# A state-space part whose decay matrices are built from rows spread by DMA and masked on GpSimd instead of by TensorE products

## The chip, the cores and the metric

The kernel is one program for one core of a Trainium2 chip. It runs three whole transformer-like blocks on 256 tokens of width 1024. The metric is the device time in microseconds, the median of several runs. TensorE (PE in the profile) multiplies matrices, VectorE (DVE) and ScalarE (ACT) do elementwise work, GpSimd (POOL) does some elementwise work and issues a few DMAs, SyncE (SP) issues all weight loads.

## The reference, cut to the state-space mixer

```python
dt = softplus(dt_raw + dt_bias); a = dt * (-exp(a_log))            # 32 heads
acum = cumsum(a)
seg  = acum[:, :, None] - acum[:, None, :]
lmat = exp(where(causal, seg, -inf))                               # decay, per head
xdt  = xc * dtc[..., None]
cb   = einsum('btgn,bsgn->btsg', cc, bc)                           # scores, per group
y    = einsum('btsg,btsgr,bsgrp->btgrp', cb, lmat, xdt)            # 8 groups of 4 heads
y    = (y + d_skip * xs) * silu(z)
y    = y * rsqrt(mean(y*y over a group) + EPS) * norm_g            # then @ w_ssd_o
```

The chunk length covers all 256 tokens, so the state terms vanish. A head is 64 channels wide, a group of four heads 256. The scores are kept with the source token on the partitions: 128 source tokens by 256 targets for the first half, 128 by 128 for the second, 384 columns in all.

## The kernel before

Everything is fp32. A weight piece of 128x1024 is split into a high and a low half: ACT copies the high half (`halves<-raw`, L2896), DVE subtracts to get the low one (L1543), and PE runs three products (hi·hi, hi·lo, lo·hi). Pieces live in a ring of four, so the high half of piece n+4 waits until PE has read piece n. Each engine has one instruction stream, executed in order, and the order is written out by hand: a wait at the head of a stream holds up all that is behind it, splits of weights included.

The part in question (`mix2`) starts when PE has finished the convolution's projection (16 tiles, pieces of L585, L586 and L589) and goes on to the gate projection `m2.gb`: eight pieces of 12 products each (L659). The state-space work is laid between these pieces in three blocks, by generators called `ssm` on PE, DVE and ACT that are advanced 22 steps before pieces 2, 4 and 6 and finished after piece 7. The first half of the gate projection fills PSUM banks 1 and 2; ACT copies them out after its split at step 3 (L3486), and piece 4 waits for it.

For each group g of four heads:

- PE computes the scores `cb` into a PSUM bank (L1150, L1151), and for each head a product with a selecting vector (L1157) that spreads the row of cumulated decays over 128 partitions, with a second product that adds the causal mask (L1158). The rows come in three parts (`acx`), made by DVE with `in_three` during the convolution.
- ACT takes the exponential with a bias from PSUM to SBUF (L3448 on 256 columns, L3449 on 128).
- DVE copies the scores to SBUF (L2328) and multiplies decay, step size and scores, two instructions a head (L2336).
- PE sums over the source tokens (L1167 to L1169, 24 products a group).
- DVE adds the skip term (L2348) and multiplies with silu(z) (L2355), ACT squares and sums (L3455), DVE finishes the mean (L2379), GpSimd raises it to the power -1/2 (`inverse_root`, L1426), DVE scales (L2362).

When all eight groups are scaled, PE transposes them (`turn` "m2.n", L567, 32 transposes), and the product with `w_ssd_o` begins (L659 with `R` as the moving side).

ACT may start its exponentials after the last silu of the convolution (L3415) and a table load (L3440). The cumulated rows are there when the scan on DVE ends (L2291), far ahead, within the convolution. SP's queue holds weight loads only, each waiting for a raw buffer.

## Time and profile before

| what | value |
|---|---|
| median of 3 runs | 2816.58 us (2816.2 to 2816.72) |
| span of the profiled execution | 2814.9 us |
| PE busy over the span | 2800.3 us, 99% |
| DVE, ACT, POOL busy | 1952.1 us, 1624.4 us, 345.9 us |
| TensorE clock granted | full in all slices |

PE is busy nearly throughout, but a product's duration is more than the step to the next one, so a busy PE isn't PE at its peak. The stretch of this change lasts from 1332.20 us (first piece of the gate projection) to 1393.27 us (first transpose) and 1397.09 us (first product of `w_ssd_o`). In a timeline a row is: start, duration, engine, line, operation, output and input, count, and in brackets the idle time ahead with what ended it.

### The profile page before, as it was taken

What the parts mean: (1) busy time and instruction counts of PE and PEld (TensorE: products, weight loads), DVE (VectorE), ACT (ScalarE), POOL (GpSimd) and SP (SyncE); (2) the same over time, 40 slices, a digit from 0 to 9 for tenths busy, and PEclk for the clock granted to TensorE, in tenths of its full rate; (3) what the DMA queues carried; (4) which work ended last, traced back from release to release, by engine and by line L of the source; (5) the groups of instructions that cost most, each with busy time, mean ns of one, the idle gap of its engine ahead of it and who ended that gap; (6) DMA issues with size and microseconds to landing.
All of it is one profiled execution on the core that took longest, in us unless ns stands there. A gap on an engine that the chain in (4) does not pass through costs nothing.

```text
span 2814.9 us, 42397 instructions
## 1 busy us (share of the span) xinstructions
PE 2800.3 (99%) x16834; PEld 2485.0 (88%) x16834; DVE 1952.1 (69%) x3377; ACT 1624.4 (58%) x2784; POOL 345.9 (12%) x314
## 2 busy tenths in 40 slices
PE   9999999999999999999999999999999999999999
PEld 7888888888988888899889999999888889988997
DVE  6657765776676676768866998677555566766775
ACT  6544655755665564566745445776555555655663
POOL 0000000000010002000002445894000000000000
PEclk9999999999999999999999999999999999999999
DMA  7554556466436555445164554434555574536454
GB/s 229 191 178 159 181 194 227 135 202 221 148 124 194 202 189 181 135 156 187 61 224 166 183 182 160 136 131 161 193 192 193 194 246 137 180 110 209 147 195 149
DMA packets 270485, 491.25 MB, mean 175 GB/s; under 512 B 10880, under 2 KB 181248, under 8 KB 261584
## 3 DMA queue, kind: packets, MB, share of 16 engines
q1 hardware_dynamic: 268864, 480.08, 51.3%
q0 software_dynamic: 1424, 8.45, 0.8%
q8 instruction: 135, 2.21, 0.3%
q14 instruction: 62, 0.51, 0.1%
HBM read 486.41 MB, written 2.10 MB: 174 GB/s over the span
## 4 chain that ended last, share of the span: by engine, by line
PE 94%; DVE 4%; ACT 1%; issue 0%; DMA 0%; POOL 0%; DVEq 0%; POOLq 0%; ACTq 0%
PE ps L659 41%; PE ps L747 11%; PE ps L589 8%; PE ps L585 8%; PE ps L586 8%; PE ps L746 6%; PE ps L606 3%; PE ps L1268 2%; DVE halves L1543 1%; PE ps L1303 1%; PE ps L544 1%; DVE AR L2499 1%; PE ps L952 0%; PE ps L1322 0%; DVE AR L2495 0%
## 5 line engine op out<-in xcount | busy, mean ns | idle before, releaser
L2896 ACT ACTIVATE halves<-raw 128x1024 fp32r<-128x1024 f32 x828 | 870.1, 1058 | 695.5 <-PE ps L659 413.7
L1543 DVE TENSOR_TENSOR halves<-raw,halves 128x1024 fp32r<-128x1024 f32 x790 | 952.9, 1227 | 190.6 <-ACT halves L2896 187.4
L659 PE MATMUL ps<-halves,XX 128*128 128x512 f32 x2628 | 611.6, 391 | 0.4
L659 PEld LDWEIGHTS ps<-halves,XX 128*128 128x128 f32 x2628 | 489.9, 188 | 102.5 <-DVE XX L1581 1.0
L585 PE MATMUL ps<-XX,halves 128*128 128x256 f32 (+1 forms) x1960 | 486.1, 286 | 0.0
L586 PE MATMUL ps<-XX,halves 128*128 128x256 f32 (+1 forms) x1960 | 480.3, 283 | 0.0
L659 PE MATMUL ps<-halves,R 128*128 128x512 f32 x1908 | 439.9, 390 | 0.1
L659 PEld LDWEIGHTS ps<-halves,R 128*128 128x128 f32 x1908 | 356.7, 188 | 73.9 <-issue 0.6
L586 PEld LDWEIGHTS ps<-XX,halves 128*128 128x128 f32 (+1 forms) x1960 | 375.4, 192 | 0.1
L585 PEld LDWEIGHTS ps<-XX,halves 128*128 128x128 f32 (+1 forms) x1960 | 375.0, 191 | 0.1
L747 PE MATMUL ps<-XX,halves 128*128 128x512 f32 x1344 | 338.4, 393 | 0.6 <-DVE XX L1581 0.6
L747 PEld LDWEIGHTS ps<-XX,halves 128*128 128x128 f32 x1344 | 241.7, 189 | 44.5 <-ACT halves L2896 0.9
L589 PE MATMUL ps<-XX,halves 128*128 128x256 f32 (+1 forms) x1960 | 275.3, 283 | 0.2 <-DVE halves L1543 0.2
L589 PEld LDWEIGHTS ps<-XX,halves 128*128 128x128 f32 (+1 forms) x1960 | 252.7, 192 | 0.4 <-DVE halves L1543 0.4
L746 PEld LDWEIGHTS ps<-XX,halves 128*128 128x128 f32 x1344 | 183.2, 190 | 13.4 <-issue 0.4
L746 PE MATMUL ps<-XX,halves 128*128 128x256 f32 x1344 | 187.5, 282 | 0.1
L1426 POOL TENSOR_TENSOR st<-st 128x1 f32<-128x1 f32 x44 | 25.3, 574 | 1182.0 <-DVE st L1608 1001.9
L1431 POOL TENSOR_TENSOR halves<-raw,halves 128x1024 fp32r<-128x1024 f32 x38 | 97.0, 2552 | 435.3 <-ACT halves L2896 435.3
L1558 DVE TENSOR_TENSOR XX<-AR,XX 128x256 fp32r<-128x256 f32 x127 | 53.9, 426 | 137.9 <-ACT XX L3579 137.9
L1509 POOL TENSOR_SCALAR raw<-iota,xsel 128x128 f32<-128x128 f32 x128 | 137.5, 1081 | 34.5 <-PE ps L1268 22.4
L1807 DVE TENSOR_TENSOR AR<-AR,ps 128x256 f32<-128x256 f32 x164 | 68.5, 421 | 81.1 <-ACT AR L3096 81.1
L3096 ACT ACTIVATE AR<-ps 128x256 f32<-128x256 f32 x164 | 61.3, 375 | 89.4 <-PE ps L747 88.0
(390 smaller groups left out, 3180.8 us busy)
## 6 DMA issues: line engine op xcount, KB each, us to landing
raw<-in_w_ffn_in SPq DMA_DIRECT2D x88, 1024.0 KB, 5.1
raw<-in_w_in SPq DMA_DIRECT2D x74, 1024.0 KB, 5.3
raw<-in_uT SPq DMA_DIRECT2D x64, 1024.0 KB, 4.9
raw<-in_peer_v SPq DMA_DIRECT2D x64, 1024.0 KB, 4.9
raw<-in_w_ffn_out SPq DMA_DIRECT2D x44, 1024.0 KB, 4.9
raw<-in_w_up SPq DMA_DIRECT2D x24, 1024.0 KB, 5.8
raw<-in_mlstm_w_in SPq DMA_DIRECT2D x12, 1024.0 KB, 5.2
raw<-in_w_down SPq DMA_DIRECT2D x12, 1024.0 KB, 4.9
```

What stands on the lines that cost most here:

```text
L585: mm(o[:, ts], hi[:, q, 0:M], xh[:, k0 + q, ts], start=first and q == 0, stop=False)
L586: mm(o[:, ts], hi[:, q, 0:M], xl[:, k0 + q, ts], start=False, stop=False)
L589: ins = mm(o[:, ts], lo[:, q, 0:M], xh[:, k0 + q, ts], start=False, stop=last and q == a - 1)
L606: ins = mm(ps[:, bs[j], :].rearrange("p (a b) -> p a b", b=128), act[q == 2][:, t, j * 128:(j + 1) * 128], k.halves[:, 0:4, q % 2, t * 128 ...
L659: ins = mm(ps[:, bs[j * (width // 512) + h], :], xv[:, k0 + t, j * 128:(j + 1) * 128], wv[:, t, h * 512:(h + 1) * 512], start=first and q ...
L746: mm(o[:, 0:256], lo[:, p, :], X[0][:, p, :], start=False, stop=False)
L747: ins = mm(o.rearrange("p (h t) -> p h t", t=256), hi[:, q, :], k.XX[:, :, q, :], start=q == 0, stop=q == 7)
L1431: nc.gpsimd.tensor_tensor(lo, src, hi.bitcast(F32), ALU.subtract).then_inc(k.lo_pool, 1)
L1509: nc.gpsimd.tensor_scalar(OA[:, g % 2, q, :], k.iota[:], ih1[:, 4 * g + q:4 * g + q + 1], gw[:, 4 * g + q:4 * g + q + 1], ALU.is_equal, AL ...
L1543: te.tensor_tensor(lo, src, hi.bitcast(F32), ALU.subtract).then_inc(k.lo_made, 1)
L1807: te.tensor_tensor(dst, dst, o[:, 0:256], ALU.add) \
L2896: act(hi, src, ACT.Copy).then_inc(k.hi_made, 1)
```

## The change

1. **Decay rows.** PE's products L1157 and L1158 are gone (64 instructions), and DVE's `in_three` with them. GpSimd writes the 32 rows of cumulated decays to HBM (two DMAs), and reads them back spread over 128 partitions, 4 rows of 384 columns a group (768 KB), into a ring of four buffers. Buffer g % 4 is refilled after PE's sums of group g - 4.
2. **Mask.** GpSimd masks each group with two `affine_select` of 128x4x128.
3. **Exponentials** read and write SBUF, eight instructions a group as before, but the four heads are marked together.
4. **Scores** are copied by ACT instead of DVE. DVE multiplies four heads at once, one instruction of 128x1536, and puts the step sizes into x, one of 128x512 (`stepped`).
5. **Scaling** of groups 0 to 5 moves from DVE to GpSimd, groups 6 and 7 stay.
6. **Order.** The generators are gone. `SSM_STEPS` says how many groups are begun by gate piece i: 0, 1, 2, 4, 5, 7, 8, 10. PE takes scores of group n and sums of group n - 2 ahead of piece i, DVE and ACT after their split for step i. Sums use the banks that the decays had, so the score banks serve scores alone.

GpSimd's stream, before (with the neighbours) and now. `AR` is the big buffer in SBUF, `rows` the new tensor in HBM; `var` is DVE's mean, `mm` PE's sums, `pow` GpSimd's own root.

```order
L1426 TENSOR_TENSOR AR<-AR,st 128x16
L1426 TENSOR_TENSOR AR<-AR,st 128x16 [waits var]
L1426 TENSOR_TENSOR AR<-AR,st 128x16
L1426 TENSOR_TENSOR AR<-AR,st 128x2 [waits var] x8
L1426 TENSOR_TENSOR st<-st 128x1 [waits x_var] x2
```

```order
L1491 DMA AR<-rows 128x1536 [waits mm]
L1497 AFFINE_SELECT AR<-AR 128x4x128 [waits dma_decay_in0]
L1497 AFFINE_SELECT AR<-AR 128x4x128
L1491 DMA AR<-rows 128x1536 [waits mm]
L1419 TENSOR_TENSOR AR<-AR,st 128x2 [waits var]
L1505 TENSOR_SCALAR AR<-AR 128x256 [waits pow]
L1505 TENSOR_SCALAR AR<-AR 128x256
L1497 AFFINE_SELECT AR<-AR 128x4x128 [waits dma_decay_in1]
L1497 AFFINE_SELECT AR<-AR 128x4x128
L1491 DMA AR<-rows 128x1536 [waits mm]
```

Eight roots in a row become a stream in which the refill of group 5 stands behind the mask of group 4, and the mask of group 5 behind root and scaling of group 0.

ACT's stream at the step of gate piece 3, before and now. L3455 (now L3486) are the squares, L3448 and L3449 (now L3467 and L3468) the exponentials, L3480 the copy of the scores, L3511 (L3486 before) the copy of gate banks 1 and 2, L2896 (now L2919) the split.

```order
L3448 ACTIVATE AR<-ps,AR 128x256 [waits mm]
L3449 ACTIVATE AR<-ps,AR 128x128
L2896 ACTIVATE halves<-raw 128x1024 [waits piece_read]
L2896 ACTIVATE halves<-raw 128x1024 [waits piece_read,raw0_in]
L3486 ACTIVATE AR<-ps 128x512 [waits piece_read]
L3486 ACTIVATE AR<-ps 128x512
L3448 ACTIVATE AR<-ps,AR 128x256 [waits mm]
```

```order
L3480 ACTIVATE AR<-ps 128x384 [waits mm,prob]
L3467 ACTIVATE AR<-AR 128x256 [waits pool]
L3468 ACTIVATE AR<-AR 128x128
L3467 ACTIVATE AR<-AR 128x256
L3468 ACTIVATE AR<-AR 128x128
L3467 ACTIVATE AR<-AR 128x256
L3468 ACTIVATE AR<-AR 128x128
L3467 ACTIVATE AR<-AR 128x256
L3468 ACTIVATE AR<-AR 128x128
L3486 ACTIVATE AR<-AR 128x256 [waits part]
L3486 ACTIVATE AR<-AR 128x256
L3511 ACTIVATE AR<-ps 128x512 [waits piece_read]
```

The wait on `pool` in the second row is the mask of group 4; squares of group 0 and the copy of the gate banks stand behind it now.

The new constants and buffers:

```diff
+SSM_STEPS = (0, 1, 2, 4, 5, 7, 8, 10)
+POOL_SCALED = 6
...
+    def decays(self, g):
+        return self.ar(8192 + g % 4 * 1536, 4, 384)
+    def stepped(self, g):
+        return self.ar(14336 + g % 2 * 512, 2, 256)
```

On PE (the rest of the old `ssm` generator is gone too):

```diff
-        def decay(h):
-            b = aux.take(pe, ("m2", "L", h))
-            mm(ps[:, b, 0:384], bc(k.sel[0:96, h:h + 1], [96, 128]), acx, start=True, stop=False)
-            ins = mm(k.diagonal(b), identb[:], mkq, start=False, stop=True)
...
+        for i, until in enumerate(SSM_STEPS):
+            for n in range(done, until):
+                if n < 8:
+                    group(n)
+                if n >= 2:
+                    sums(n - 2)
```

On GpSimd:

```diff
+    def spread(g):
+        if g >= 4:
+            gp.wait_ge(*k.full["m2", "ssm", g - 4])
+        load(k.decays(g), k.rows[4 * g:4 * g + 4, :].partition_broadcast(128))
+    def masked(g):
+        gp.wait_ge(*dma[f"decay_in{g % 4}"].need(g))
+        for o in (0, 256):
+            L = k.decays(g)[:, :, o:o + 128]
+            ins = nc.gpsimd.affine_select(L, L, [[0, 4], [1, 128]], ALU.is_ge, NEG, base=0, channel_multiplier=-1)
+    for g in range(4):
+        spread(g)
+    for g in range(4):
+        masked(g)
+    for g in range(9):
+        if g < 4:
+            spread(g + 4)
+        if g:
+            n = 2 * g - 2
+            inverse_root(cc[:, 144 + n:146 + n], cc[:, 128 + n:130 + n], s["var"].need(("m2.g", g - 1)), ("m2.g", g - 1))
+        if 1 <= g <= POOL_SCALED:
+            scaled(g - 1)
+        if g < 4:
+            masked(g + 4)
```

On DVE, whose order for each n is: `group(n)`, `sums(n - 2)`, `stepped(n)`, `moment(n - 3)`, and `scale(n - 4)` from n = 10 on:

```diff
-            for j, o in enumerate((slice(0, 256), slice(256, 384))):
-                ins = te.scalar_tensor_tensor(L[:, o], L[:, o], cc[:, 32 * j + h:32 * j + h + 1],
-                                              cbs[:, h // 4 % 2, o], ALU.mult, ALU.mult)
+            te.tensor_tensor(k.decays(g), k.decays(g), bc(cbs[:, g % 2, :].unsqueeze(1), [128, 4, 384]), ALU.mult)
```

On ACT:

```diff
+        def ssm(n):
+            if n < 8:
+                score(n)
+            if n < 7:
+                group(n + 1)
+            if 3 <= n < 11:
+                sums(n - 3)
...
+        group(0)
+        for i, until in enumerate(SSM_STEPS):
             weights()
+            for n in range(done, until):
+                ssm(n)
```

## Rows read from the trace of the kernel before

**Rows 1.** The page: busy time of each engine over the span

```profile
PE 2800.3 (99%) x16834; PEld 2485.0 (88%) x16834; DVE 1952.1 (69%) x3377; ACT 1624.4 (58%) x2784; POOL 345.9 (12%) x314
```

**Rows 2.** Windows: length, busy time by engine (instructions), clock, DMA share, GB/s

```profile
1300.00:1332.00 32.00, 32.00 (x269) 32.00 (x268) 26.25 (x45) 19.20 (x27) 0.00 (x0) 1.00 0.61 200
1332.20:1393.27 61.07, 59.88 (x386) 51.20 (x385) 54.26 (x150) 39.74 (x112) 5.81 (x8) 1.00 0.22 70
1393.27:1397.09 3.82, 3.74 (x34) 3.41 (x32) 3.82 (x7) 3.75 (x11) 0.00 (x0) 1.00 0.03 8
```

**Rows 3.** Timeline of PE in the stretch

```profile
1332.20 5.63 PE L659 MATMUL ps<-halves,XX 128*128 128x512 f32 x24
1337.67 0.59 PE L1150 MATMUL ps<-AR 128*128 128x256 f32 x2
...
1338.24 0.42 PE L1157 MATMUL ps<-R,sel 96*128 96x384 f32 x1
...
1338.55 0.42 PE L1157 MATMUL ps<-R,sel 96*128 96x384 f32 x1
...
1342.92 0.33 PE L1167 MATMUL ps<-AR 128*128 128x64 f32 x2
...
1345.54 0.65 PE L1150 MATMUL ps<-AR 128*128 128x256 f32 x2
```

**Rows 4.** Groups, 1337 to 1400 us: count, busy, mean ns, idle before

```profile
L3448 ACT ACTIVATE AR<-ps,AR 128x256 f32<-128x256 f32 x32 | 15.8, 492 | 11.3 <-PE ps L1158 11.3
L2336 DVE SCALAR_TENSOR_TENSOR AR<-AR 128x256 f32<-128x256 f32 x32 | 15.4, 480 | 1.9 <-ACT AR L3449 1.1
...
L2348 DVE SCALAR_TENSOR_TENSOR AR<-AR,ps 128x128 f32<-128x128 f32 x32 | 8.9, 343 | 0.8 <-PE ps L1169 0.8
...
L1426 POOL TENSOR_TENSOR AR<-AR,st 128x2 f32<-128x2 f32 x8 | 5.8, 726 | 279.4 <-DVE AR L2379 279.4
L2355 DVE TENSOR_TENSOR AR<-AR 128x512 f32<-128x512 f32 x8 | 5.5, 692 | 0.3
```

**Rows 5.** Timeline of ACT around its first exponentials and the gate copy

```profile
1336.58 1.28 ACT L3440 ACT_TABLE_LOAD   x1
...
1337.98 1.99 ACT L2896 ACTIVATE halves<-raw 128x1024 fp32r<-128x1024 f32 x2
1339.88 0.46 ACT L3448 ACTIVATE AR<-ps,AR 128x256 f32<-128x256 f32 x1
...
1340.49 0.47 ACT L3448 ACTIVATE AR<-ps,AR 128x256 f32<-128x256 f32 x1
...
1357.98 1.08 ACT L3486 ACTIVATE AR<-ps 128x512 f32<-128x512 f32 x2 [1.59 <-PE ps L659]
...
1359.56 0.43 ACT L3455 ACTIVATE AR<-AR 128x256 f32<-128x256 f32 x1
...
1360.27 0.22 ACT L3455 ACTIVATION_READ_ACCUMULATOR AR<-AR 128x1 f32 x1
```

**Rows 6.** GpSimd's lines: duration in ns, min/median/max

```profile
L1511 POOL TENSOR_SCALAR raw<-iota,xsel x64: 595/598/1681, 1734.3 to 1939.4; 128x128 f32<-128x128 f32 x64
...
L1431 POOL TENSOR_TENSOR halves<-raw,halves x38: 2397/2410/3717, 12.1 to 2593.0; 128x1024 fp32r<-128x1024 f32 x38
```

**Rows 7.** Timelines of GpSimd and DVE where both run

```profile
1745.76 2.58 POOL L1509 TENSOR_SCALAR raw<-iota,xsel 128x128 f32<-128x128 f32 x2 [0.52 <-PE ps L1268]
...
1753.30 1.65 POOL L1509 TENSOR_SCALAR raw<-iota,xsel 128x128 f32<-128x128 f32 x2 [0.81 <-PE ps L1268]
...
1746.37 1.22 DVE L1543 TENSOR_TENSOR halves<-raw,halves 128x1024 fp32r<-128x1024 f32 x1
```

**Rows 8.** The page and the DMA view: KB each, median us from issue to landing

```profile
spill<-AR POOLq DMA_DIRECT2D x1, 1024.0 KB, 5.2
...
AR<-in_rpack POOLq DMA_DIRECT2D x2, 512.0 KB, 7.0
```

**Rows 9.** Timeline of DVE: the scan that gives the decay rows

```profile
1272.11 0.69 DVE L2291 TENSOR_TENSOR_SCAN AR<-AR 96x256 f32<-96x256 f32 x1
```

More of the change, by code:

```diff
@@ L317, in __init__ @@
         (self.raw, self.halves, self.AR, self.part_at, self.XX, self.XF, self.cols, self.ident,
[L318 removed]
+         self.identb, self.sel, self.iota, self.mask, self.st, self.xsel, self.first, self.ps, self.spill, self.rows) = mem
         self.X = (self.XX[:, 0], self.XX[:, 1])
@@ L1200, in mix2 @@
                     k.full["m2.gb", s0, j] = k.piece_read, n + 1
-        pe.finish()
-        turn("m2.n", xs, lambda c, j: s["chan"].need(("m2", c // 2, j)), n=16, banks=k.late)
+        turn("m2.n", xs, lambda c, j: (s["pool"] if c // 2 < POOL_SCALED else s["chan"]).need(("m2", c // 2, j)),
+             n=16, banks=k.late)
         mix = k.ar(17408, 2, 1024)
@@ L2292, in dt_rows @@
             yield
-            acx = k.part_at(26112, 384)[0:96, :]
-            v.wait_ge(*step.need("m2.rows"))
-            in_three(acx[:, 0:256], ac)
             yield
-            te.tensor_copy(acx[:, 256:384], acx[:, 128:256].bitcast(F32)).then_inc(*step.mark("m2.acx"))
             yield
@@ L3442, in decay, with group, score @@
         def decay(h):
[L3443 to L3450 removed]
+            L = k.decays(h // 4)[:, h % 4, :]
+            act(L[:, 0:256], L[:, 0:256], ACT.Exp, bias=cc[:, 64 + h:65 + h])
+            return act(L[:, 256:384], L[:, 256:384], ACT.Exp, bias=cc[:, 96 + h:97 + h])
+        def group(g):
+            a.wait_ge(*s["pool"].need(("m2.L", g)))
+            a.wait_ge(*aux.gone(("m2", "cols")))
+            ins = [decay(h) for h in range(4 * g, 4 * g + 4)][-1]
+            ins.then_inc(*s["act"].mark(("m2.L", g)))
+        def score(g):
+            if g >= 2:
+                a.wait_ge(*s["prob"].need(("m2.L", g - 2)))
+            a.wait_ge(*full["m2", "cb", g])
+            act(cbs[:, g % 2, :], ps[:, k.right.of(("m2", "cb", g)), 0:384], ACT.Copy) \
+                .then_inc(*k.right.done(("m2", "cb", g)))
         def sums(g):
```

179 lines of the change are left out of this document (73 added, 106 removed).

## The prediction

> **What bounds the kernel now.** The page comes first: PE is busy for 99% of the span [rows 1], so the question is what the one stretch that changes costs PE. The windows give its length: 61.07 us from the first gate piece to the first transpose and 3.82 us of transposes, 64.89 us together; PEclk stands at 1.00, so the clock plays no part, and GpSimd does 5.81 us in all of it [rows 2]. PE's timeline gives the steps, not the durations, since products overlap. Two gate pieces take 1337.67 - 1332.20 = 5.47 us, so 2.74 each; scores of a group 1338.24 - 1337.67 = 0.57; a head's decay pair 1338.55 - 1338.24 = 0.31; a group's sums 1345.54 - 1342.92 = 2.62 [rows 3]. So PE's own work before the transposes is 8 x 2.74 + 8 x 0.57 + 32 x 0.31 + 8 x 2.62 = 21.9 + 4.6 + 9.9 + 21.0 = 57.4 us of 61.07. DVE is busy for 54.26 of the 61.07, ACT for 39.74 [rows 2]: near its end PE is paced by DVE, which waits little. ACT does wait, 11.3 us for PE's masked rows [rows 4].
>
> **What goes.** The decay pairs leave PE: 9.9 us, and with them most of the remaining 3.7 us of waits could go. PE's floor becomes 47.5 us, 13.6 us under today; that is the most that this change could give. DVE loses the multiplications per head (15.4 us for the 256-column form alone [rows 4]), the score copies and six scalings, and gets per group one product of 1536 columns and one of 512. The latter is 0.69 [rows 4]; 1024 columns take 1.22 [rows 7], so a column costs 1.03 ns and 1536 of them about 1.75 us, an estimate. 8 x 2.44 = 19.5 us: DVE stops being a bound by its own work. ACT gets eight score copies of about 0.5 us. `in_three` leaves DVE in the convolution, where PE has no idle time in a window of 32.00 us [rows 2]: worth nothing.
>
> **What hides.** The rows are ready at 1272.8 [rows 9], 59 us ahead of the stretch. Two stores, four refills and eight masks fit in there: even at the dearest prices below, one after the other (5.2 for the stores as for a 1024 KB one [rows 8], 4 x 8, 8 x 2.4), that is 56 us. The refills add 3 MB to weight loads with DMA share 0.61 [rows 2]; I cost that at nothing, because ACT and not the transfer paces the splits there. If the cover failed, it would cost the few us by which a weight load came late.
>
> **What comes on the path.** Only groups 0 to 3 are prepared ahead. For 4 to 7 the order on GpSimd and ACT makes a chain, which I follow from t = 0 at 1332.20.
>
> (a) ACT used to split right behind the table load, at 1337.98 [rows 5], t = 5.8. Now the exponentials of group 0 stand there: 4 x 0.61 = 2.44 (1340.49 - 1339.88 a head), then two splits, 1.90 [rows 5]. DVE's product of group 0 stands behind the split of a piece that needs the first of these, and needs ACT's score copy behind both: 5.8 + 2.4 + 1.9 + 0.5 = 10.6. Product 1.75, step sizes 0.69, sums 2.62: 15.7, with five handovers of 0.1 us 16.2. PE has nothing else by then and idles about 3 us.
>
> (b) The refill of group 4 waits for these sums. 768 KB: 1024 KB from the same queue took 5.2 us, two spread rows of 512 KB together 7.0 [rows 8]. I take 5.5, nearer the single transfer, range 4.5 to 8. Then the mask, which no row shows. A 128x128 tensor-scalar takes 0.60 us; 128x1024 with two inputs takes 2.41, half of that is 1.2 for 512 columns [rows 6]. Bounds for one instruction are 0.6 (as the 128-column one) and 2.4 (four times that); I take 1.1, so 2.2 a group. Group 4 is masked at t = 16.2 + 5.5 + 2.2 = 23.9.
>
> (c) ACT stands at the exponentials of group 4 meanwhile. Behind them in its stream are the squares of group 0 and the copy of the gate banks, for which PE waits with piece 4. And on GpSimd the mask of group 5 stands behind root and scaling of group 0, which need those squares. So from mask to mask the path is: exponentials 2.5, squares 0.9 (1359.56 to 1360.49 [rows 5]), mean 0.16, root 0.73 [rows 4], two scalings of 256 columns of about 0.8 (0.6 for 128 [rows 6], and twice the columns), mask 2.2, handovers 0.5: 8.6 us. The refill beside it is 5.5 + 2.2 = 7.7, just shorter. Three such periods lead to group 7.
>
> (d) GpSimd slows beside DVE. A pair of its instructions took 1.65 us alone and 2.58 with one DVE subtraction of 1.22 us in it [rows 7]: 0.9 us. DVE is in instructions with two SBUF inputs for about half of this stretch, so I add 1.0 us to each period and to the first mask.
>
> Mask 7 ends at 23.9 + 1.0 + 3 x 9.6 = 53.7.
>
> (e) Then exponentials 2.5, squares 0.9, split 1.0, score copy 0.5, product 1.75, and ahead of the step sizes of group 7 DVE has four skip additions (1.1) and one product (0.69) [rows 4], then the step sizes 0.69: with handovers 9.6, t = 63.3. Sums 2.62, piece 7 2.74: 68.7. Transposes 3.8, and 0.5 for gate banks that ACT empties late: 73.0.
>
> Against 64.89 that is +8.1 us. The same counting on the old order came out 1 to 2 us above its trace, so my handovers are a little dear; I take +7. Nothing outside the stretch changes. The profiled span was 2814.9 us against a median of 2816.58; the difference of 1.7 stays, so 2816.6 + 7 = **2823.6 us**.
>
> **Two pages against the rows.** That two DVE and GpSimd instructions disturb each other is in [rows 7]. The Trainium skill, SBUF — State Buffer, section "SBUF: two separate sides", has it that the shared port pair is an exclusive lock held for a whole instruction, against DVE instructions with two SBUF inputs. The stretched pair agrees with that; taken to the letter, a mask would wait for all of a 1.75 us product, and the sum would be about +10. The Trainium skill, GPSIMD Engine Reference, section "Performance versus the Vector engine", gives 769 ns for 512 elements in its best case; masks at that price would be 0.7 us cheaper a group and the sum about +4.
>
> **The rivals.**
>
> *It becomes faster.* GpSimd decides: four masks and three periods lie on the path. If the two masks of a group cost 1.2 us (the lower bound) and DVE doesn't slow them, a period is 7.6 and the first mask ends at 22.9; mask 7 ends at 45.7, 8 us ahead of the forecast, and PE's own queue (s4 to s7 with pieces 5 to 7) takes up half of it: -1 to -4 us, 2813.5. The point at which it turns is a period of about 7.6 to 7.8 us instead of 9.6. For it speaks that only exponentials and squares, 3.4 us, are fixed; against it, [rows 7]. Chance 0.12.
>
> *Masks as I price them, little contention.* Subtract 1.0 x 4 us and the handovers: +2 to +4, 2819.5. For it: root and scaling are short, and DVE itself waits in each period. Chance 0.30.
>
> *The refill decides.* If 768 KB spread over partitions takes 8 us (two of 512 KB together took 7.0), the first mask comes 2.5 us later, and each period is 10.2 + 1.0 of contention instead of 9.6: +14, 2831. Chance 0.12.
>
> *The mask is dear.* At 2.4 us an instruction, 2.6 more for each of four groups: +17, 2834. Chance 0.08.
>
> Forecast: 0.38.
>
> **How the numbers follow.** A measurement of this kernel tells 0.2%, 5.6 us, from no change. The forecast's own spread is +4 to +11, with 0.27 of its 0.38 above 5.6; with both dear cases this gives slower 0.47. The little-contention case and the rest are within, and most of the gain in the fast rival is too (its far end of -4 isn't enough, so a real gain needs more than I count): same 0.43, faster 0.10. The range reaches from the fast rival to the refill case, 2813 to 2833.
>
> **What would show it.** Right: PE has no L1157 or L1158 rows; it idles before the first sums, before gate piece 4 (waiting for ACT's copy) and most before the last sums, 6 us or more; ACT waits three or four times for GpSimd, 3 to 6 us each; GpSimd's masks come 9 to 10 us apart. DVE idles where it was full. Wrong: masks below 0.7 us or a period below 8 us; a refill above 7 us; PE waiting before the first four groups, which would mean that the preparation isn't hidden; or idle time of PE within the convolution.

## The result, and the profile after

| | before | after |
|---|---|---|
| median, us (4 runs each) | 2816.65 | 2831.26 |
| lowest to highest, us | 2816.2 to 2816.85 | 2831.18 to 2833.16 |
| profiled span, us | 2814.9 | 2829.4 |
| mean granted clock | 1.0 | 0.994 |

The changed kernel is slower by 14.6 us: a ratio of 1.0054 (from the single runs, not from the two medians), 95% interval 1.004 to 1.0068. The forecast was 2823.6 in a range of 2813 to 2833: the direction and the range held, the forecast loss of 7 us was half of what came.

All of it lies in the stretch that the prediction followed. Below are the windows of the changed kernel (length, busy time of PE, PEld, DVE, ACT, POOL with instructions, granted clock, DMA share, GB/s): the convolution ahead of the stretch, the stretch up to the first transpose, and the transposes up to the first product of `w_ssd_o`.

```profile
1300.00:1332.00 32.00, 32.00 (x269) 32.00 (x268) 26.26 (x44) 18.96 (x27) 0.00 (x0) 1.00 0.64 206
1331.96:1406.35 74.39, 61.95 (x323) 55.27 (x322) 47.39 (x78) 43.56 (x116) 33.77 (x31) 0.79 0.34 114
1406.35:1411.75 5.40, 3.94 (x34) 3.38 (x32) 2.98 (x10) 5.20 (x16) 0.72 (x1) 1.00 0.00 0
```

Against [rows 2] the convolution is as full of PE work as before and ends at the same time (1331.96, before 1332.20): the preparation of four groups is hidden. The stretch has grown from 61.07 to 74.39 us and the transposes from 3.82 to 5.40: 79.79 against 64.89, 14.9 us more. Up to the first transpose DVE has lost 6.9 us of work (54.26 to 47.39) and GpSimd has gained 28 us (5.81 to 33.77). New, and foreseen in no step, is the third column from the right, the granted clock: 0.79 where it was 1.00. Finer windows of the same kernel show where:

```profile
1348.00:1356.00 8.00, 8.00 (x36) 7.82 (x36) 7.38 (x11) 6.18 (x17) 1.58 (x3) 0.50 0.62 207
1356.00:1361.00 5.00, 5.00 (x14) 3.87 (x14) 3.70 (x7) 3.10 (x10) 2.37 (x2) 0.53 0.48 193
1361.00:1388.00 27.00, 22.52 (x155) 20.32 (x153) 16.59 (x26) 12.22 (x36) 18.61 (x17) 1.00 0.29 99
1388.00:1400.00 12.00, 6.93 (x34) 6.78 (x34) 8.42 (x17) 7.40 (x24) 7.31 (x6) 0.50 0.06 4
```

PE's timeline names what went ahead of each fall (start, duration, and in brackets the wait ahead with its releaser):

```profile
1342.92 0.70 PE L1162 MATMUL ps<-AR 128*128 128x256 f32 x2 [1.25 <-ACT AR L3480]
...
1345.48 0.41 PE L1173 MATMUL ps<-AR 128*128 128x64 f32 x2 [1.64 <-DVE AR L2362]
...
1355.56 5.38 PE L671 MATMUL ps<-halves,XX 128*128 128x512 f32 x12
...
1364.03 3.01 PE L671 MATMUL ps<-halves,XX 128*128 128x512 f32 x12
...
1387.30 0.41 PE L1173 MATMUL ps<-AR 128*128 128x64 f32 x2 [3.59 <-DVE AR L2362]
...
1397.07 0.66 PE L1173 MATMUL ps<-AR 128*128 128x64 f32 x2 [5.07 <-DVE AR L2362]
...
1402.18 4.33 PE L671 MATMUL ps<-halves,XX 128*128 128x512 f32 x12
```

PE waits 1.25 us for ACT's first score copy and 1.64 for the step sizes of group 0; 1.8 us later, within the sums of group 0, its granted clock falls to the lower level, 1.2 GHz, and the fourth gate piece takes 5.38 us where the next takes 3.01. Ahead of the sums of groups 6 and 7 it waits 3.59 and 5.07 us, and again runs at half clock: the sums of group 7 last from 1397.07 to 1402.18 (5.1 us for 2.6), the last piece 4.33.

GpSimd's timeline, from the first refill inside the stretch on:

```profile
1349.71 0.55 POOL L1491 DMA_DIRECT2D AR<-rows  x1 [58.08 <-PE ps L1175]
1354.97 2.89 POOL L1497 TENSOR_SCALAR_AFFINE_SELECT AR<-AR 128x512 f32<-128x512 f32 x2 [4.72 <-DMA AR<-rows]
1357.81 0.56 POOL L1491 DMA_DIRECT2D AR<-rows  x1
1361.86 1.62 POOL L1419 TENSOR_TENSOR AR<-AR,st 128x2 f32<-128x2 f32 x1 [3.49 <-DVE AR L2393]
1363.59 2.92 POOL L1505 TENSOR_SCALAR AR<-AR 128x256 f32<-128x256 f32 x2
1366.47 1.67 POOL L1497 TENSOR_SCALAR_AFFINE_SELECT AR<-AR 128x512 f32<-128x512 f32 x2
...
1376.70 1.67 POOL L1497 TENSOR_SCALAR_AFFINE_SELECT AR<-AR 128x512 f32<-128x512 f32 x2
...
1385.98 1.67 POOL L1497 TENSOR_SCALAR_AFFINE_SELECT AR<-AR 128x512 f32<-128x512 f32 x2
```

Here is the chain of step (c): refill, mask, a wait for the mean (which ACT's exponentials and squares precede), root, two scalings, next mask. The masks end at 1357.86, 1368.14, 1378.37 and 1387.65, so 10.3, 10.2 and 9.3 us apart. The list of waits (what waited, for what, us in total, times, longest) shows the other side of it:

```profile
POOL AR L1419 <- DVE AR L2393: 19.9, 7, 4.0
ACT AR L3467 <- POOL AR L1497: 18.5, 4, 5.2
DVE AR L2393 <- ACT AR L3486: 17.6, 5, 4.2
...
PE ps L1173 <- DVE AR L2362: 11.2, 4, 5.1
...
POOL AR L1497 <- DMA AR<-rows: 4.7, 1, 4.7
```

ACT waits four times for masks, DVE five times for ACT's squares, PE four times for DVE's step sizes. GpSimd waits for a refill once only, for group 4; the later refills had landed while it stood at its roots.

### The profile page after: what moved, and what is told of

Same layout as the page of the kernel before. It is cut to its first block, busy times and chain, and to the rows that moved or that the text cites. A ratio compares the mean times of both kernels' runs of the same rounds, so it can differ in the third digit from the quotient of the medians.

```text
span 2829.4 us, 42262 instructions
## 1 busy us (share of the span) xinstructions
PE 2803.3 (99%) x16770; PEld 2489.2 (88%) x16770; DVE 1941.9 (69%) x3301; ACT 1628.5 (58%) x2792; POOL 383.9 (14%) x352
## 4 chain that ended last, share of the span: by engine, by line
PE 92%; DVE 4%; ACT 2%; issue 1%; POOL 1%; DMA 0%; DVEq 0%; POOLq 0%; ACTq 0%
PE ps L671 39%; PE ps L759 11%; PE ps L601 8%; PE ps L597 8%; PE ps L598 8%; PE ps L758 6%; PE ps L618 3%; PE ps L1261 2%; DVE halves L1573 1%; PE ps L1296 1%; PE ps L556 1%; DVE AR L2522 1%; PE ps L964 0%; PE ps L1315 0%; DVE AR L2518 0%
## 5 line engine op out<-in xcount | busy, mean ns | idle before, releaser
L2919 ACT ACTIVATE halves<-raw 128x1024 fp32r<-128x1024 f32 x828 | 869.6, 1058 | 697.5 <-PE ps L671 413.0
L1539 POOL TENSOR_SCALAR raw<-iota,xsel 128x128 f32<-128x128 f32 x128 | 137.5, 1081 | 34.6 <-PE ps L1261 22.5
```

The costliest lines, as they stand in the source:

```text
L1539: nc.gpsimd.tensor_scalar(OA[:, g % 2, q, :], k.iota[:], ih1[:, 4 * g + q:4 * g + q + 1], gw[:, 4 * g + q:4 * g + q + 1], ALU.is_equal, AL ...
L2919: act(hi, src, ACT.Copy).then_inc(k.hi_made, 1)
```

## What could have caused it

**Mine:** the chain of handovers between GpSimd and ACT sets the end, as in the forecast, and the waits that it leaves on PE take PE's clock, which makes the work behind them dearer. **Rivals:** the clock costs nothing, since PE waits for others anyway; the refill decides, and the chain only follows it (the prediction's rival at 2831 us, next to the measured time); DVE or ACT has become the bound.

In every experiment the "stretch" is the time from the first gate piece to the first product of `w_ssd_o` in the profiled execution. These are the windows of all stretches, one row each, in the order of the runs: kernel after, e1_warm, e2_masks_first, e3_vector_scales, e4_squares_first, e5_warm_longer, e6_six_buffers, e7_six_squares_first, e8_six_squares_warm, e9_two_places_later, e10_third_mask, e11_early_product, e12_steps_first.

```profile
1331.96:1411.75 79.79, 65.89 (x355) 58.64 (x353) 50.37 (x88) 48.76 (x132) 34.48 (x32) 0.81 0.32 106
1332.37:1410.73 78.36, 73.61 (x478) 66.80 (x476) 49.78 (x88) 48.78 (x132) 32.62 (x32) 0.93 0.31 108
1331.94:1410.32 78.38, 65.59 (x354) 58.49 (x353) 49.56 (x88) 48.76 (x132) 30.29 (x32) 0.80 0.31 108
1331.81:1405.40 73.59, 63.38 (x354) 56.37 (x353) 52.05 (x100) 48.77 (x132) 20.45 (x20) 0.84 0.32 115
1332.05:1405.93 73.88, 65.69 (x354) 58.74 (x353) 49.82 (x88) 48.86 (x132) 29.60 (x32) 0.82 0.33 114
1332.11:1405.83 73.72, 70.78 (x493) 64.65 (x492) 49.95 (x88) 48.78 (x132) 32.81 (x32) 1.00 0.33 115
1334.63:1398.61 63.98, 59.63 (x355) 53.27 (x353) 49.13 (x88) 48.68 (x132) 30.69 (x26) 0.89 0.32 107
1333.63:1397.65 64.02, 59.67 (x355) 53.63 (x353) 49.24 (x88) 48.79 (x132) 28.58 (x26) 0.89 0.31 107
1333.18:1394.36 61.18, 58.20 (x382) 52.17 (x380) 49.24 (x88) 48.59 (x132) 29.32 (x26) 0.97 0.33 112
1331.92:1393.38 61.46, 58.49 (x381) 52.30 (x380) 49.54 (x88) 48.67 (x132) 29.23 (x26) 0.97 0.33 112
1332.22:1416.80 84.58, 68.36 (x355) 60.98 (x353) 50.54 (x88) 48.76 (x132) 36.53 (x36) 0.78 0.28 100
1331.75:1395.05 63.30, 60.10 (x368) 53.96 (x367) 48.78 (x88) 48.78 (x132) 30.28 (x26) 0.92 0.31 109
1331.79:1390.99 59.20, 56.17 (x375) 50.18 (x373) 48.51 (x88) 49.46 (x135) 30.44 (x26) 1.00 0.34 116
```

| kernel | median (lowest to highest, runs), us | ratio to before, 95% | stretch, us | clock in it |
|---|---|---|---|---|
| before | 2816.65 (2816.2 to 2816.85, 4) | 1 | 64.89 | 1.00 |
| after | 2831.26 (2831.18 to 2833.16, 4) | 1.0054 (1.0040 to 1.0068) | 79.79 | 0.81 |
| e1 | 2829.68 (2828.51 to 2831.65, 4) | 1.0044 (1.0028 to 1.0061) | 78.36 | 0.93 |
| e5 | 2825.68 (2825.29 to 2826.01, 6) | 1.0031 (1.0019 to 1.0044) | 73.72 | 1.00 |
| e2 | 2829.51 (2828.47 to 2830.22, 4) | 1.0044 (1.0028 to 1.0061) | 78.38 | 0.80 |
| e3 | 2826.64 (2825.02 to 2828.55, 5) | 1.0038 (1.0023 to 1.0052) | 73.59 | 0.84 |
| e4 | 2824.26 (2823.55 to 2827.92, 10) | 1.0028 (1.0019 to 1.0038) | 73.88 | 0.82 |
| e10 | 2836.55 (2833.95 to 2836.91, 4) | 1.0068 (1.0051 to 1.0084) | 84.58 | 0.78 |
| e6 | 2818.28 (2816.66 to 2820.54, 10) | 1.0004 (0.9994 to 1.0014) | 63.98 | 0.89 |
| e7 | 2817.32 (2816.53 to 2818.71, 10) | 1.0002 (0.9992 to 1.0011) | 64.02 | 0.89 |
| e8 | 2813.98 (2812.81 to 2815.48, 10) | 0.9990 (0.9980 to 0.9999) | 61.18 | 0.97 |
| e9 | 2811.85 (2811.09 to 2812.93, 10) | 0.9983 (0.9973 to 0.9993) | 61.46 | 0.97 |
| e11 | 2813.08 (2811.13 to 2814.80, 10) | 0.9987 (0.9978 to 0.9997) | 63.30 | 0.92 |
| e12 | 2811.64 (2810.62 to 2813.78, 11) | 0.9983 (0.9974 to 0.9992) | 59.20 | 1.00 |

The kernel before, run beside each of these, had medians between 2816.53 and 2816.88; the ratios are to its runs on the same chip.

## Experiment 1: PE kept busy in its waits

```diff
+FILL = {"cb": 10, 0: 13, "gate": 26, 5: 6, 6: 28, 7: 40}
...
+        def fill(g, n):
+            if g not in taken:
+                taken[g] = aux.take(pe, ("m2", "ssm", g))
+            for _ in range(n):
+                mm(ps[:, taken[g], 0:256], X[0][:, 0, 0:128], X[0][:, 1, :], start=True, stop=True)
...
         def sums(g):
-            b, xd = aux.take(pe, ("m2", "ssm", g)), k.stepped(g)
+            fill(g, FILL.get(g, 0))
+            b, xd = taken[g], k.stepped(g)
```

> The changed kernel, and in front of each of PE's long waits of the stretch products of 256 columns whose results nobody reads (10, 13, 26, 6, 28 and 40 of them, about 0.12 us each): before the third scores 1.2 us, the first sums 1.6, the fifth gate piece 3, the sums of groups 5, 6 and 7 0.7, 3.4 and 4.7. Nothing else differs. In the changed kernel PE's granted clock stands at 0.5 from 1348 to 1361 and from 1388 to 1400, after waits, and the stretch from the first gate piece to the first product of w_ssd_o takes 79.8 us. My theory (chain of handovers plus lost clock): the clock stays at 1.0, the masks come as far apart as now, and the stretch loses what half clock cost on the path, 2.2 us in the first sums and the gate piece behind them and 3 to 4 us in the last sums, the last piece and the transposes: 74 to 76 us, and 2825 to 2827 us in all (the changed kernel: 2831.3). Rival (the clock costs nothing, since PE waits for others anyway): the clock rises and the time stays, 2831 within 1 us. Second rival (PE falls to half clock for another reason than its waits): the rows still show 0.5 and the time stays or grows.

Measured: 2829.68 us, 1.6 less than after and outside the 2825 to 2827 that were expected, a stretch of 78.36 instead of 79.79. The clock stayed at 1.0 until the sums of group 7, as expected; then it fell, and with it most of the gain. That PE still waited there, 2.07 us, decided a second run with more of the same:

```diff
-FILL = {"cb": 10, 0: 13, "gate": 26, 5: 6, 6: 28, 7: 40}
+FILL = {"cb": 10, 0: 13, "gate": 26, 5: 6, 6: 28, 7: 56}
```

> The run with products in front of PE's waits (e1_warm), with 56 instead of 40 of them ahead of the sums of group 7. There PE still waited 2.07 us after the 40, and its clock stood at 0.5 in the last sums, the last gate piece and part of the transposes (5.3 us for sums that take 2.9 at full clock, 5.4 for a piece that takes 2.9). If the wait is what takes the clock, as I hold, the clock stays at 1.0 to the end and the stretch falls from 78.4 to 73 to 74 us: the total, 2829.7 there, to 2824 to 2826. Rival (the clock falls for another reason, or its loss in the tail is hidden behind GpSimd's last scalings, which the transposes need): 2829 to 2831. The chain of handovers itself is not touched: the last mask comes at about 51.5 us after the first gate piece, as in e1_warm.

Measured: 2825.68 us and a stretch of 73.72, 6.1 us less than after. PE's timeline at the sums of group 7, of e1_warm:

```profile
1387.90 5.04 PE L1173 MATMUL ps<-XX 128*128 128x256 f32 x40
1395.01 0.56 PE L1183 MATMUL ps<-AR 128*128 128x64 f32 x2 [2.07 <-DVE AR L2376]
...
1400.02 5.47 PE L672 MATMUL ps<-halves,XX 128*128 128x512 f32 x12
```

and of e5_warm_longer:

```profile
1387.80 6.95 PE L1173 MATMUL ps<-XX 128*128 128x256 f32 x56
1394.91 0.41 PE L1183 MATMUL ps<-AR 128*128 128x64 f32 x2 [0.16 <-DVE AR L2376]
1397.58 3.02 PE L672 MATMUL ps<-halves,XX 128*128 128x512 f32 x12
```

The pair is the cleanest evidence of this study. The sums of group 7 start at the same time, 1395.01 and 1394.91; the only difference is whether PE worked or waited for the 2 us ahead of them. With the wait the first product of `w_ssd_o` comes at 1410.73, without it at 1405.83: 4.9 us, all behind the chain, 2.3 of it in the sums and 2.4 in the last piece (5.47 us for 3.02). The transposes take 5.4 us in both. These are two single executions; the medians of the two kernels are 4.0 us apart. So a wait on PE costs twice: while it lasts, and in what PE does next. The rival that the clock costs nothing falls. The Trainium skill, TensorE: Matmul & The Clock Gate, section "Part 1: The HAM clock gate (the "warmup" mystery)", says that this clock is lowered when the engine is idle; these rows agree with it.

What is left at full clock is what the change costs without the clock, the chain and the tail behind it: 73.72 - 64.89 = 8.8 us. So of the 14.9 us of the stretch 6.1 are the clock's and 8.8 the rest's, of which 1.6 are transposes (5.4 us for 3.8). In the total 2831.26 - 2825.68 = 5.6 us are the clock's.

## Experiment 2: links taken out of the chain

Three runs take one link each out of the way from mask to mask. The masks ahead of root and scaling, on GpSimd:

```diff
         if g < 4:
             spread(g + 4)
+            masked(g + 4)
...
-        if g < 4:
-            masked(g + 4)
```

> The changed kernel with one order turned on GpSimd: the masks of group g+4 stand right behind its refill, ahead of root and scaling of group g-1. Chain of handovers (mine): a mask no longer waits for squares, mean, root and scaling of an earlier group, only for its refill, 5.4 us behind the sums; ACT's exponentials of groups 5 to 7 start 2 to 4 us earlier each, but root and scaling then stand behind a mask that waits for a refill. In sum 2 us less by the handovers and up to 4 more where PE waits too little to lose its clock: 2825 to 2830 us. Rival (the refill decides): mask starts come no closer together than now, 10 us, and the time is 2831 within 1 us. Slower than 2832 would mean that the scaled groups, which the transposes need, come late.

Measured: 2829.51 us, 1.75 less than after: within the expectation, but little. GpSimd's timeline of e2_masks_first shows why:

```profile
1366.29 0.71 POOL L1419 TENSOR_TENSOR AR<-AR,st 128x2 f32<-128x2 f32 x1
1367.11 2.69 POOL L1505 TENSOR_SCALAR AR<-AR 128x256 f32<-128x256 f32 x2
1369.76 0.63 POOL L1491 DMA_DIRECT2D AR<-rows  x1
1374.77 1.90 POOL L1497 TENSOR_SCALAR_AFFINE_SELECT AR<-AR 128x512 f32<-128x512 f32 x2 [4.38 <-DMA AR<-rows]
```

Root and scaling went out of the way of the mask, but they now stand ahead of the next refill's issue, on the same queue, and for groups 5 to 7 GpSimd then waits 3.9 to 4.4 us for the transfer (7.1 for group 4): the refill took their place in the chain. Here it is the refill that decides; in the changed kernel it isn't.

The scalings on DVE:

```diff
-POOL_SCALED = 6
+POOL_SCALED = 0
```

> The changed kernel with the scalings of all eight groups on DVE (0.6 us a pair on paper, an estimate from 0.60 for 256 columns of one operand twice at most) instead of six of them on GpSimd, where a pair takes 2.8 to 2.9 us beside DVE. Chain of handovers (mine): each of the three periods from mask to mask (10.2 us) loses the pair, 2.9 us, until the refill (5.4 plus mask 1.7) or ACT sets it: mask 7 comes 6 to 8 us earlier, PE's last waits shrink, and the total is 2822 to 2825 us. Rival (DVE becomes the bound: the scalings stand ahead of products that PE waits for): the periods stay near 10 us and the time at 2830 or above. Rival (the refill decides): less than 1 us.

Measured: 2826.64 us, 4.6 less than after and short of what was expected (6 to 9 less), the stretch 6.2 less. The masks end 8.3, 8.2 and 7.2 us apart. One row of e3's GpSimd timeline tells why it isn't more:

```profile
1370.78 3.44 POOL L1497 TENSOR_SCALAR_AFFINE_SELECT AR<-AR 128x512 f32<-128x512 f32 x2
```

A pair of masks that takes 1.67 us at this place in the changed kernel takes 3.44 beside two scalings, a low half and a product of DVE: what left GpSimd's list came back in part as disturbance. DVE was no bound (busy 52.05 of 73.59 us).

The squares ahead of the exponentials on ACT:

```diff
             if n < 8:
                 score(n)
-            if n < 7:
-                group(n + 1)
             if 3 <= n < 11:
                 sums(n - 3)
+            if n < 7:
+                group(n + 1)
```

> The changed kernel with one order turned on ACT: the squares of group n-3 stand ahead of the exponentials of group n+1, which wait for GpSimd's mask, instead of behind them. Chain of handovers (mine): squares, mean, root and scaling of a group now run while the mask is still waited for, so that a period loses the exponentials (2.8) and the squares (0.9) as links ahead of the next mask; the handovers alone give 7 to 8 us, and a mask comes every 7 to 8 us: 2821 to 2825 us. Rival (GpSimd's own work and DVE's disturbance of it set the period): GpSimd does 2.9 + 1.7 + 1.6 + 0.6 = 6.8 us a period, so less than 3 us is left to gain, and the time is 2828 or above. Rival (the refill decides): 2831 within 1.

Measured: 2824.26 us, 7.0 less than after, as expected: the order of two blocks on ACT, with no instruction added or taken, is worth half of the change's whole loss. The masks end 5.7, 10.2 and 6.2 us apart. The rival that GpSimd's own work sets the period (less than 3 us to gain) falls, and so does the refill for the changed kernel: here the one of group 4 even took longer (GpSimd waited 6.4 us for it, 4.7 in the changed kernel).

The opposite, a link made longer:

```diff
+        if g >= 4:
+            L = k.decays(g)[:, :, 128:256]
+            ins = nc.gpsimd.affine_select(L, L, [[0, 4], [1, 128]], ALU.is_ge, NEG, base=128, channel_multiplier=-1)
         ins.then_inc(*s["pool"].mark(("m2.L", g)))
```

> The changed kernel with a third masking instruction of 512 columns for each of groups 4 to 7, over the block that needs no mask (its condition holds everywhere, so it changes no value). Alone such an instruction takes 0.62 us, beside DVE up to 1.3. Chain of handovers (mine): the masks lie in the chain one to one, so four times 0.6 to 1.3 us are added, 2.5 to 4 us: 2834 to 2835.5, and the masks come 10.8 to 11.3 us apart instead of 10.2 and 9.3. Rival (GpSimd has slack and the refill or ACT sets the period): 2831 to 2832 and unchanged distances.

Measured: 2836.55 us, 5.3 more than after (expected 2.5 to 4). The third masks took 1.08, 1.08, 0.63 and 0.63 us in its trace, 3.4 in all; the ends of group 4's and group 7's masks are 32.0 us apart instead of 29.8. In this execution PE's clock had also fallen earlier in the first sums, so that the first refill left at 19.2 us after the first gate piece instead of 17.8. With 3.4 for the masks and 1.4 for the later refill this is 4.8, the growth of the stretch, in part by luck: the refill of group 4 also took 1.6 us longer than in the changed kernel, and its first two masks 1.2 less (1.67 for 2.89). Between the masks of groups 4 and 7 the account is clean: 2.3 us of added masks, 2.2 us more. There they lie in the chain one to one.

## Experiment 3: the chain taken away

Six places for decay rows instead of four; groups 4 and 5 are prepared within the convolution too. The squares' unread output, which lay on one of the new places, goes onto scores' inputs that are no longer needed.

```diff
     def decays(self, g):
-        return self.ar(8192 + g % 4 * 1536, 4, 384)
+        return self.ar((8192, 9728, 11264, 12800, 23552, 30720)[g % 6], 4, 384)
...
-        if g >= 4:
-            gp.wait_ge(*k.full["m2", "ssm", g - 4])
+        if g == 4:
+            gp.wait_ge(*k.full["m2", "cols"])
+        if g >= 6:
+            gp.wait_ge(*k.full["m2", "ssm", g - 6])
```

> The changed kernel with six instead of four places for the decay rows: the rows of groups 4 and 5 are spread and masked before the stretch too, so that only groups 6 and 7 go through the chain of refill and mask inside it (the squares' unused output goes to the scores' inputs, since its old place holds rows). Orders on ACT, DVE and GpSimd are otherwise those of the changed kernel. Chain of handovers (mine): ACT's exponentials of groups 4 and 5 wait for nothing, those of 6 and 7 for masks that need the sums of groups 0 and 1 only; the three periods of 10 us are gone, and the stretch takes what PE, ACT and DVE do by themselves, about 58 us by the handovers, and 2 to 5 more for waits and clock in its first third: 60 to 63 us instead of 79.8, the total 2811 to 2815, that is below the kernel before (2816.6). Rival (DVE and ACT are the bound in this form, whatever GpSimd does): no better than the orders tried, 73 to 74 us, 2824 or above. Rival (two more refills of 768 KB ahead disturb the weight loads of the convolution): the stretch shrinks but time is lost before it.

Measured: 2818.28 us, 13.0 less than after and no different from before. The stretch is 63.98 us; expected were 60 to 63. With two masks instead of four left inside the stretch the form reaches the old one, which none of the runs with four places did. The 13.0 us aren't the chain's alone: PE no longer waits ahead of the sums of groups 6 and 7, and the clock stays at 1.00 there, which was worth 4.9 us between e1 and e5. Most of the miss was the third rival: PE waits once inside the convolution (waits of PE in e6_six_buffers, 1240 to 1335 us; then its window of the refills):

```profile
PE ps L1143 <- ACT AR L3440: 2.1, 1, 2.1
```

```profile
1276.00:1296.00 20.00, 20.00 (x170) 20.00 (x169) 12.09 (x21) 7.43 (x12) 13.79 (x18) 1.00 1.04 380
1296.00:1306.00 10.00, 7.87 (x65) 7.53 (x64) 7.72 (x15) 8.68 (x13) 0.53 (x1) 1.00 0.54 167
```

With six refills in a row the DMA share stands at 1.04 for 20 us, ACT waits 8.4 us in one place for a weight piece (3.1 us in the changed kernel), ACT and DVE are busy for only 7.43 and 12.09 us of the 20, and the first gate piece comes at 1334.63 instead of 1331.96.

The order on ACT with the chain gone, the edit of e4 on top of e6:

```diff
             if n < 8:
                 score(n)
-            if n < 7:
-                group(n + 1)
             if 3 <= n < 11:
                 sums(n - 3)
+            if n < 7:
+                group(n + 1)
```

> Six places as in e6_six_buffers, and the squares ahead of the exponentials on ACT as in e4_squares_first. If the order of squares and exponentials matters only because it is a link of the chain through the masks, as I hold, then with the chain gone it is worth within 1.5 us of e6_six_buffers, where it was worth 7 with four places. Rival (the order matters by itself, since it brings the scalings forward): 3 us or more faster than e6_six_buffers.

Measured: 2817.32 us and 64.02 us of stretch, within 1.0 us of e6. The same edit gave 7.0 us with four places: nearly all of its worth was that of a link of the chain.

Then PE kept busy in its first three waits:

```diff
+FILL = {"cb": 10, 0: 13, "gate": 0, 1: 4}
```

> e7_six_squares_first with products that nobody reads in front of PE's waits for the third scores (10), the first sums (13) and the second sums (4). With four places the same products ahead of the first sums kept the clock at 1.0 where it fell to 0.5, and brought the fourth gate piece from 23.6 to 20.3 us after the first. If PE in the six-place form is still late by this piece when the stretch ends, the total falls by 2 to 3 us against e7_six_squares_first; rival (DVE paces the rest of the stretch, and PE only waits later instead): within 0.7 us of it.

Measured: 2813.98 us, 3.3 less than e7, a stretch of 61.18: a little more than expected. And the refills of groups 4 and 5 apart from each other and from the first four:

```diff
+        if g in (4, 5):
+            gp.wait_ge(*s["act"].need(("m2.conv", 8 * g - 20)))
...
-    for g in range(6):
-        spread(g)
-    for g in range(6):
-        masked(g)
+    for g in range(4):
+        spread(g)
+    for g in range(4):
+        masked(g)
+    for g in (4, 5):
+        spread(g)
+        masked(g)
```

> e8_six_squares_warm with the refills of groups 4 and 5 issued later: each waits for the convolution's tiles 12 and 20, instead of all six going out in a row at 1275.6. With six in a row the DMA share stood at 1.03 to 1.05 from 1276 to 1296 and PE waited 0.6 us in one place of the convolution (2.1 us in e6_six_buffers), so that the first gate piece began 1.2 to 2.6 us later than in the kernel before. If the crowd of refills delays a weight load, the wait in the convolution goes, the first gate piece starts at 1332 again, and the total falls by about 1 us against e8 (2814.0) to 2812.5 to 2813.5. Rival (the wait comes from somewhere else, the start being the rival): the gate piece still starts at 1333 or later and the total stays within 0.5 us.

Measured: 2811.85 us, 2.1 less than e8, more than the 0.5 to 1.5 expected (e8 ran on another chip, on which the kernel before took 0.35 us more), and 4.7 less than before (ratio 0.9983, 0.9973 to 0.9993). The stretch is the same, 61.46; it starts at 1331.92 again, and PE has no wait in the convolution. So the crowd of refills was the cause of that wait.

## Experiment 4: the head of the stretch

In e9 one dip of the clock was left; PE's timeline of e9_two_places_later:

```profile
1359.90 4.58 PE L672 MATMUL ps<-halves,XX 128*128 128x512 f32 x12 [1.31 <-ACT AR L3532]
```

A wait of 1.31 us for the gate banks, and the piece takes 4.58 instead of 3.0. Three orders were turned at once to get rid of this and of the first waits, and the unread products changed with them (none before the third scores, 8 before the first sums, 6 before the second):

```diff
         a.wait_ge(*s["act"].need(("m2.conv", 30)))
+        score(0)
         group(0)
...
+                if c == 0:
+                    group(4)
...
-        for until in SSM_STEPS:
+        for until in (1,) + SSM_STEPS[1:]:
             weights()
```

> e9_two_places_later with three orders turned at the head of the stretch: ACT copies the first scores ahead of the first exponentials; DVE multiplies group 0 ahead of the low halves of the piece behind (they wait for ACT anyway); and ACT empties the gate banks ahead of the exponentials of group 4, since PE waited 1.3 us for them with the fifth piece and then ran it at half clock (4.4 us). Fewer unread products (8 and 6). By the handovers the first sums come 2.3 us earlier (11.2 instead of 13.5 us after the first gate piece), the second 1 to 2, the fifth piece 3 us, of which the clock is 1.5. If PE's first waits set the end of the stretch: 58 to 59 us instead of 61.2, the total 2810 to 2812. Rival (DVE paces the middle of the stretch, 0.4 us of idle time between its products): the early gain is lost again by group 4, and the total is within 1 us of e9.

Measured: 2813.08 us, 1.2 more than e9. The first sums did come 2.0 us earlier (11.5 us after the first gate piece). Then, after waits of 0.24 and 0.63 us and with only 6 unread products, the clock stood at 0.50 from 1347.5 to 1350, and the fourth piece came no earlier than in e9. The fifth came 1.1 us earlier and at full clock, the seventh 2.4, and all of it was lost at the end, as the rival said, though by another place than DVE alone (PE's timeline of e11_early_product):

```profile
1380.89 0.41 PE L1183 MATMUL ps<-AR 128*128 128x64 f32 x2 [0.86 <-DVE AR L2383]
1385.74 4.07 PE L672 MATMUL ps<-halves,XX 128*128 128x512 f32 x12
```

A wait of 0.86 us for the step sizes of group 7 stands ahead of sums that take 4.9 us and a piece that takes 4.07. These step sizes stood behind four additions and the gate on DVE. In the last run the two are turned round, and 12 instead of 6 unread products stand before the second sums:

```diff
-FILL = {"cb": 0, 0: 8, "gate": 0, 1: 6}
+FILL = {"cb": 0, 0: 8, "gate": 0, 1: 12}
...
             if n < 8:
+                stepped(n)
+            if 2 <= n < 10:
                 sums(n - 2)
-            if n < 8:
-                stepped(n)
```

> e11_early_product with the step sizes of a group ahead of the skip additions of the group two before on DVE, and 12 instead of 6 unread products before the second sums. In e11 the sums of group 7 waited 0.86 us for their step sizes, which stood behind 1.8 us of additions and gate on DVE; PE then ran these sums and the last gate piece at half clock (5.1 and 4.1 us for 2.9 and 3.0). If that is why e11 gave nothing over e9, the sums of group 7 now start by 48 us after the first gate piece and the clock stays at 1.0: a stretch of 58.5 to 60 us against 61.5 and 63.3, and 2809 to 2811 us in all. Rival (DVE, which is busy without a gap from group 5 to 7, sets the end in any order): 61 us or more and no faster than e9, 2811.9.

Measured: 2811.64 us over 11 runs, above the 2809 to 2811 expected. The profiled execution, at 2810.62 us the fastest of them, has a stretch of 59.20 us with the clock at 1.00 throughout and the sums of group 7 at 47.4 us, so the mechanism holds in it; which of the two edits did how much isn't separated. The median is only 0.2 us under e9's, inside the scatter of both (the other executions of e12 reach 2813.78). That e12 is better than e9 isn't shown. Both are about 5 us faster than the kernel before, with intervals that end at 0.9993 and 0.9992.

## Why the prediction was right or wrong

Times from the first gate piece (t = 0), as in the prediction:

| step | forecast | after | e5 (clock at 1.0) |
|---|---|---|---|
| (b) mask of group 4 ends | 24.9 | 25.9 | 22.5 |
| (c, d) mask of group 7 ends | 53.7 | 55.7 | 53.4 |
| (e) sums of group 7 start | 63.3 | 65.1 | 62.8 |
| first transpose | 68.7 | 74.4 | 68.3 |
| first product of `w_ssd_o` | 73.0 | 79.8 | 73.7 |

**What goes, what hides: right.** There are no decay pairs on PE. DVE's product took 1.76 us where nothing disturbed it, as worked out from its neighbours (1.75). Two stores, four refills and the first four pairs of masks ended at 1291.6, 40 us ahead of the stretch, and PE had no wait there. The preparation isn't free in larger doses: six refills in a row cost 2.1 us (e6).

**(a) Right until the clock.** PE waited where it was foreseen, 1.25 and 1.64 us (forecast about 3), and began the first sums at 13.5. They ended at 17.4 instead of 16.2, because the clock fell under them; at full clock (e5) they ended at 16.4.

**(b) Right for the changed kernel.** A refill took 4.6 us by the median of the four inside the stretch (forecast 5.5, range 4.5 to 8). The first one wasn't as steady: 6.8 to 7.5 us to landing in e2, e4, e7 and e10, near the forecast's sign "a refill above 7 us"; why isn't known.

**(c) and (d) Right in the mechanism, the terms off in both directions.** A period was forecast at 9.6 and took 10.3, 10.2 and 9.3. In it, the exponentials took 2.75 to 2.8 instead of 2.5, the root 1.62 instead of 0.73 twice out of three, the two scalings 2.8 to 2.9 instead of 1.6, and the masks 1.67 instead of 2.2; these hold the 1.0 us that was set aside for the disturbance. A masking instruction of 512 columns takes 0.62 us (1.24 a pair at 1281.29), the lower bound. So one sign of being wrong came, "masks below 0.7 us", and yet the period wasn't short, since beside DVE the rest of it was dearer. Had GpSimd been undisturbed, the fast rival's period of 7.6 would have been near, by an estimate from these rows: root 0.73, scalings 1.83 and masks 1.24 are 2.4 us less than what stood there.

**(e) Right up to its last line.** Mask 7 to the sums of group 7 took 9.4, forecast 9.6. Then came the failed step: "Sums 2.62, piece 7 2.74" took 5.1 and 4.2, together 9.3 instead of 5.4. The transposes with their gate banks took 5.4 instead of 4.3, which isn't the clock's: they take 5.4 in e5 too. ACT empties the gate banks (1406.55) ahead of the last squares, so root and scaling of group 7 come late.

**The step that failed** is in the first paragraph: "PEclk stands at 1.00, so the clock plays no part". This was read from a stretch in which PE hardly waits, and carried over to a form that, by the forecast itself, makes PE wait 3 us at the head and 6 or more at the end. In its sum the term at nothing is what the waits do to the products behind them. The same sum at full clock is e5's column: 73.7 against 73.0. The clock's 6.1 us were missing. That e5 comes so near is partly luck: the mask of group 4 ends 2.4 us before its forecast, the three periods are 11.4, 10.2 and 9.3 instead of 9.6 each (in the first, the mean waits 1.4 us behind other work of DVE), and the transposes are 1.1 longer. The second, smaller error was to take 1.1 us off the sum, from 8.1 to 7, for handovers that were "a little dear", after a counting on the old order of which no row is shown; at full clock it came to 8.8.

**The rivals.** The refill case named 2831 us, nearly the measured time, and was wrong: only one mask waited for a refill, 4.7 us, and e4 gained 7 us without touching a refill. A number that fits is no evidence for its mechanism. "Masks as I price them, little contention" fell with the root at 1.62 and the scalings at 2.9. The dear mask fell at once. The form can be faster than before, but not by a cheap GpSimd: it takes most of the chain out of the stretch, which alone gives no difference (e6, e7), and PE kept busy besides (e8, e9, e11, e12). One sign of being right didn't come: a wait ahead of gate piece 4. At half clock PE reached this piece after ACT's copy; at full clock, in e8 and e9, it waits 1.31 us there.

**The two pages.** The first pair of masks inside the stretch and the product beside it, GpSimd's row above and DVE's here:

```profile
1355.18 2.19 DVE L2355 TENSOR_TENSOR AR<-AR 128x1536 f32<-128x1536 f32 x1
```

The masks began at 1354.97 and took 2.89 us for two of 0.62 each. Together, 1.24 of masks and 1.76 of product are 3.0 us, and both were done by 1357.86. The second mask began at 1355.72, inside the product, and took 2.14 us, to 0.49 us behind its end. This is what one gets if they ran one after the other, the product held by the first mask and the second mask by the product. The rule of the Trainium skill, SBUF — State Buffer, section "SBUF: two separate sides", by which the port is held for a whole instruction, agrees with these two rows. Other rows don't follow it to the letter: the root of 0.73 us at 1382.37 and the product of 1.76 us at 1382.55 overlap for 0.55 us, and neither is longer than alone (in e5 likewise). The forecast's sum of about +10 by this rule counted a whole product for every mask; only one of the four pairs met a product in full, and the stretch without the clock's part came to +8.8. The 769 ns for 512 elements of the Trainium skill, GPSIMD Engine Reference, section "Performance versus the Vector engine", called a best case there, is above the 0.62 us measured for a masking instruction of 512 columns; the measurement decides.

## What to carry to other kernels

Count what a new wait on TensorE does to the work behind it: price the products after each new wait at full and at half clock, and take a trace's clock of 1.00 only for forms in which the engine waits as little as there. Where two engines feed each other through in-order queues, write down what stands in one period of the loop; moving one block past a wait (squares ahead of exponentials, 7 us) or a deeper ring (13 us, what the clock gives back in both included) was worth more than making a member of the loop faster (4.6 us), and once most of the loop was gone the same reordering gave 1.0 us, too little to tell from nothing. Spread prefetches over the time that is there: the same six transfers cost 2 us when issued in a row and nothing when two of them were held back.

## What the runs showed of the hardware that was not expected

- The granted clock of TensorE was 0.50 after waits of 1.25 and 1.64 us close together, after 2.07, after 3.59 and 5.07, and in parts also after single waits of 1.31 us (piece of 4.58 us for 3.0) and of 0.86 (sums of 4.9 us for 2.7). It stayed at 1.00 with waits up to 0.52 us (e5). The length of a wait doesn't decide alone: after 0.89 us ahead of the sums of group 5 and 1.16 ahead of `w_ssd_o` in the changed kernel the clock stayed at 1.00, and in e11 it fell after 0.24 and 0.63. Nor does it fall at the same point each time: after the same 1.25 and 1.64 us the first refill left at 17.6 to 19.2 us (after, e2, e3, e4, e10), as the fall came later or earlier in the first sums. The work was 128x64 products in most of these places; how much the small products have to do with it wasn't tried.
- Products with an unread result, 139 in all in e5, held it at 1.00 and made the changed kernel 5.6 us faster.
- Small GpSimd instructions are stretched beside DVE as much as large ones: a root of 256 values took 1.62 us instead of 0.72 beside a DVE subtraction of 1.22 us, two scalings 2.9 instead of 1.83, two masks up to 3.44 instead of 1.24.
